# Two blocks of a transformer on one core: modulation chunks placed anew in the feed-forwards and between them

## The reference, cut to what matters

```python
c_act = jax.nn.silu(c)
for i in range(DEPTH):                       # 2
    mod = c_act @ mod_w[i] + mod_b[i]        # 9 * 1024 columns
    sh1, sc1, g1, sh2, sc2, g2, sh3, sc3, g3 = jnp.split(mod, 3 * N_SUB, axis=-1)
    h = modulate(rmsnorm(x, norm_g[i, 0]), sh1, sc1)
    x = x + FFN_RES * g1[:, None, :] * swiglu(h, ffn_w13[i, 0], ffn_w2[i, 0])
    h = modulate(rmsnorm(x, norm_g[i, 1]), sh2, sc2)
    m = pool_ssd_mixer(h, ...) if i % 2 == 0 else mla_mixer(h, ...)
    x = x + g2[:, None, :] * m
    h = modulate(rmsnorm(x, norm_g[i, 2]), sh3, sc3)
    x = x + FFN_RES * g3[:, None, :] * swiglu(h, ffn_w13[i, 1], ffn_w2[i, 1])
```

## Time and profile before

| | |
|---|---|
| median of 3 runs | 1763.58 us (1763.45 to 1764.44) |
| span of the profiled execution | 1764.7 us |
| TensorE busy | 1669.9 us, 95% |
| VectorE busy | 1290.2 us, 73% |
| ScalarE busy | 933.4 us, 53% |
| POOL busy | 86.6 us, 5% |
| first feed-forward, its SiLUs | 54.1 to 238.1 us |
| second feed-forward | 408.8 to 592.2 us |
| third feed-forward | 613.9 to 796.8 us |
| granted TensorE clock 0.50 before 1300 us | 3.4 us each from 82.9, 437.9 and 642.7 us |

### The profile page before, as it was taken

One profiled execution on the slowest core, in us unless ns is written; L12 is line 12 of the kernel. 1 busy time (PEld: TensorE's weight loads), 2 busy tenths in 40 slices (PEclk: granted clock), 3 DMA queues, 4 the chain that ended last, 5 costly groups with the idle time before them and its releaser, 6 DMA issues.

```text
span 1764.7 us, 31956 instructions
## 1 busy us (share of the span) xinstructions
PE 1669.9 (95%) x11230; PEld 1500.6 (85%) x11230; DVE 1290.2 (73%) x2161; ACT 933.4 (53%) x1664; POOL 86.6 (5%) x151
## 2 busy tenths in 40 slices
PE   6899999999999999999999999999988899999998
PEld 5899989888999889998777888898976789988886
DVE  6888888768888888876566666679888565456665
ACT  1544457644444544445575555555467845555553
POOL 2000010300000100000000000000000000000000
PEclk9999999999999999999999999999999999999999
DMA  8888866757888888865433766444633155446561
GB/s 348 311 295 297 306 173 204 156 203 249 300 292 307 236 293 302 294 184 175 131 108 70 240 191 185 148 148 151 186 97 91 49 191 168 143 136 198 191 184 65
DMA packets 123657, 352.76 MB, mean 200 GB/s; under 512 B 9851, under 2 KB 52875, under 8 KB 114225
## 3 DMA queue, kind: packets, MB, share of 16 engines
q1 hardware_dynamic: 108128, 262.18, 46.4%
q10 hardware_dynamic: 12432, 78.65, 13.8%
q0 software_dynamic: 3008, 10.74, 1.9%
HBM read 347.31 MB, written 4.22 MB: 199 GB/s over the span
## 4 chain that ended last, share of the span: by engine, by line
PE 55%; DVE 20%; issue 11%; ACT 8%; DMA 4%; ACTq 1%; POOL 1%; DVEq 0%; POOLq 0%; SPq 0%
PE ps L829 36%; PE ps L1062 8%; PE ps L1063 4%; DVE w_lo L195 4%; DVE arena L358 4%; DVE arena L2680 2%; ACT w_hi L1116 2%; ACT w_hi L189 2%; DVE w_lo L1127 1%; DMA gate_scratch<-gcol 1%; DMA resid<-in_x 1%; DVE resid L1322 1%; DVE act_s L1196 1%; DMA grow<-gate_scratch 1%; ACTq L332 1%
## 5 line engine op out<-in xcount | busy, mean ns | idle before, releaser
L829 PE MATMUL ps<-t_both,w_hi 128*128 128x256 f32 x3952 | 725.9, 285 | 10.1 <-DVE t_both L758 5.7
L829 PEld LDWEIGHTS ps<-t_both,w_hi 128*128 128x128 f32 x3952 | 615.0, 191 | 23.5 <-issue 10.6
L829 PE MATMUL ps<-t_both,w_lo 128*128 128x256 f32 x1976 | 558.5, 283 | 1.3 <-issue 1.3
L195 DVE TENSOR_TENSOR w_lo<-raw,w_hi 128x1024 fp32r<-128x1024 f32 x240 | 288.6, 1222 | 122.6 <-ACT w_hi L189 122.4
L829 PEld LDWEIGHTS ps<-t_both,w_lo 128*128 128x128 f32 x1976 | 376.6, 191 | 0.2
L1127 DVE TENSOR_TENSOR w_lo<-raw,w_hi 128x1024 fp32r<-128x1024 f32 x258 | 313.6, 1221 | 83.0 <-ACT w_hi L1116 82.9
L1116 ACT ACTIVATE w_hi<-raw 128x1024 fp32r<-128x1024 f32 x258 | 268.8, 1053 | 120.2 <-PE ps L829 79.2
L189 ACT ACTIVATE w_hi<-raw 128x1024 fp32r<-128x1024 f32 x240 | 248.2, 1053 | 143.1 <-PE ps L829 99.6
L1062 PE MATMUL ps<-t_both,w_hi 128*128 128x512 f32 x640 | 226.7, 398 | 0.0
L829 PE MATMUL ps<-w_hi,g_hi 128*128 128x512 f32 x440 | 176.8, 402 | 14.4 <-DVE g_lo L1199 11.9
L1063 PE MATMUL ps<-t_both,w_lo 128*128 128x256 f32 x640 | 179.7, 281 | 0.0
(11 more groups left out here) (378 smaller groups left out, 1662.4 us busy)
## 6 DMA issues: line engine op xcount, KB each, us to landing
raw<-in_stream SPq DMA_DIRECT2D x498, 512.0 KB, 4.5
arena<-in_mod_w ACTq DMA_DIRECT2D x72, 1024.0 KB, 7.2
grow<-gate_scratch POOLq DMA_DIRECT2D x6, 512.0 KB, 7.7
u_scratch<-u_keep ACTq DMA_DIRECT2D x1, 3072.0 KB, 36.8
arena<-u_scratch POOLq DMA_DIRECT2D x8, 256.0 KB, 3.3
small<-in_small POOLq DMA_DIRECT2D x1, 1368.0 KB, 11.2
resid<-in_x POOLq DMA_DIRECT2D x1, 1024.0 KB, 18.9
arena<-in_mem POOLq DMA_DIRECT2D x1, 1024.0 KB, 5.4
```

Of the source, the lines that this page charges most:

```text
L195: VE.tensor_tensor(w_lo[:, s, :], raw[:, s, :], w_hi[:, s, :].bitcast(F32), ALU.subtract).then_inc(lo_done, 1)
L829: last = TE.matmul(out, lhs, rhs, start=start and i == 0, stop=stop and i == 2)
```

## The change

Chunks are placed anew. The first feed-forward keeps 4 to 14 in its bodies 0 to 10, but its last body now has the ordinary order of products, and the fold of chunk 14; the chunk's gather, copy and add come behind the narrow product that opens the mixer (`mod_finish`). Chunk 15 starts one split earlier in the mixer's output product (6 to 9 in place of 7 to 9), is folded behind the ninth, and its gather stands behind the tenth block. The second feed-forward has no chunk in body 0, chunks 16 to 25 in bodies 1 to 10, and loads chunk 26 in its last body. The third has no chunk in body 0 (it gathers chunk 25 there), and 26 to 35 in bodies 1 to 10; chunk 35 ends behind the narrow product that opens the second mixer. `late_mod`, `late_load`, `next_mod`, the products in `squares`, the turn in `turn` and `mod_add` are gone. Body 1 of the second and third is written out, and the loop runs over bodies 2 to 9. The first mixer's narrow turn now waits for the copy of chunk 14 (`mod_taken`), since both use bank 7. Nothing of the computation is left out.

```diff
+        def mod_finish(c, place):
+            @block.tensor
+            def _(pe):
+                mod_gather(pe, c, PRE, place)
+            @block.scalar
+            def _(act):
+                mod_take(act, c, PRE, place)
+            @block.gpsimd
+            def _(pool):
+                mod_place(pool, c, PRE)
...
             diag_at[0] = (ready[0, 1], A.n)
             square(1, 1)
             root(1)
-            if late_mod is not None:
-                @block.vector
-                def _(dve):
-                    mod_products(dve, late_mod, (6, 7), turns_at[late_mod])
-
...
-                if late_mod is not None:
-                    @block.tensor
-                    def _(pe):
-                        pe.wait_ge(V.sem, added[QT - 1, 1])
-                        mod_turn(pe, late_mod, place=L)
-
-                    @block.vector
-                    def _(dve):
-                        mod_add(dve, late_mod, turns_at[late_mod], place=L)
-                    if late_load:
-                        mod_first(late_mod + 1, place_free=True, halves=(1,))
...
                 opening = static and i == 0
+                late = static and i == FG - 1
                 for t in range(2):
-                    closing = t == 1 and static and i == FG - 1
-                    if mod is not None and not opening and not closing:
+                    if mod is not None and not opening:
                         mod_products(dve, mod, range(4 * t, 4 * t + 2), turns)
...
-                    if mod is not None and closing:
-                        mod_products(dve, mod, range(4 * t, 4 * t + 2), turns)
-                    elif mod is not None and t == 1 and not opening:
+                    if mod is not None and t == 1 and not opening:
                         mod_products(dve, mod, range(4 * t + 2, 4 * t + 4), turns)
...
-                if mod is not None and not (late and late_mod):
+                if mod is not None:
                     mod_fold(dve, mod, turns)
...
-                owing = 0 < lo and n_mod and lo <= n_mod
+                mod = mod_bodies and lo >= mod_bodies[0]
+                owing = mod_bodies and lo > mod_bodies[0] or call == 2 and lo == 0
...
+            loop_at = 2 if mod_bodies and mod_bodies[0] else 1
+            for i in range(loop_at):
+                if i == 0 and mod_bodies:
+                    blocks["hi"] = h0 + RING
+                emit(i, i + 1)
+            emit(loop_at, FG - 1)
+            if residual is not None:
+                gate_row(residual)
+            emit(FG - 1, FG)
...
         narrow_product(16, ps[2], ahead=4)
+        mod_finish(PRE + FG - 1, L)
         narrow_at, dt_read = A.n, [0]
...
                     pe.wait_ge(A.sem, narrow_at)
+                    pe.wait_ge(mod_taken, FG)
...
-            if between[0] in (7, 8, 9):
+            if between[0] in (6, 7, 8, 9):
                 @block.vector
                 def _(dve):
-                    mod_products(dve, PRE + FG, range(2 * between[0] - 14, 2 * between[0] - 12), turns_at[PRE + FG])
+                    mod_products(dve, PRE + FG, range(2 * between[0] - 12, 2 * between[0] - 10), PRE)
+                    if between[0] == 9:
+                        mod_fold(dve, PRE + FG, PRE)
+            if between[0] == 10:
+                mod_finish(PRE + FG, 0)
...
-        mod_first(PRE + FG + 1, place_free=True, halves=(0,))
+        mod_first(PRE + FG + 1, place_free=True)
...
-        ffn(1, FG, PRE + FG + 1, (mod_at(0, 8), 0.5), next_mod=PRE + 2 * FG + 1)
+        ffn(1, range(1, FG), PRE + FG + 1, (mod_at(0, 8), 0.5), load_on=True)
-        ffn(2, N_MOD - PRE - 2 * FG - 1, PRE + 2 * FG + 1, (mod_at(1, 2), 0.5))
+        ffn(2, range(1, FG), PRE + 2 * FG, (mod_at(1, 2), 0.5))
...
         narrow_product(32, ps[2], ahead=4)
+        mod_finish(N_MOD - 1, L)
```

More of the change, by code:

```diff
@@ L378, in mod_fold, with mod_gather @@
             VE.tensor_reduce(mod_lanes[:, :], mod_swap.rearrange("p (b r) -> p b r", r=32), AX, ALU.add).then_inc(mod_summed, 1)
-        def mod_gather(pe, c, turns):
+        def mod_gather(pe, c, turns, place=0):
             n = c - turns
@@ L393, in mod_take @@
                 rows = slice(32 * g, 32 * g + 32)
-                last = E.activation(mod_sum[rows, :], ps[7][rows, g:16:4], ACT.Copy)
+                last = E.activation(mod_sum[rows, :], ps[7][rows, place + g:place + 16:4], ACT.Copy)
             last.then_inc(mod_taken, 1)
@@ L1017, in _, with ffn @@
                     mod_load(act, half, c)
-        def ffn(call, n_mod, mod0, residual, next_mod=None):
+        def ffn(call, mod_bodies, mod0, residual, load_on=False):
             h0 = blocks["pe"]
@@ L1027, in ffn @@
             fresh = turned["at"] == (V.n, A.n)
-            late_mod = n_mod == FG
-            wide = n_mod == 0
+            wide = not mod_bodies
             sb0 = 2 * (FG - 1) * (call - 3)
-            turns = (PRE, PRE + 2, PRE + 3, None, None)[call]
+            turns = PRE
             def slot(j):
@@ L1243, in _ @@
                         with act.Fori(lo, hi) as i:
-                            act_body(act, i, False, mod_of(i), True, owed_of(i) if owing else None)
+                            act_body(act, i, False, mod_of(i), True, owed_by(i))
                     else:
                         m = mod_of(lo)
-                        act_body(act, lo, True, m, m is not None and lo + 1 < n_mod, owed_of(lo) if owing else None)
+                        act_body(act, lo, True, m, m is not None and (lo + 1 < FG or load_on), owed_by(lo))
                 @block.vector
@@ L1261, in _ @@
                             with pool.Fori(lo, hi) as i:
-                                mod_place(pool, owed_of(i), turns)
+                                mod_place(pool, owed_by(i), turns)
                         else:
-                            mod_place(pool, owed_of(lo), turns)
-            def with_mod(i):
-                return i + mod0
-            def no_mod(i):
-                return None
-            if n_mod:
-                blocks["hi"] = h0 + RING
-                emit(0, 1, with_mod)
-                if n_mod == FG:
-                    emit(1, FG - 1, with_mod)
-                    if residual is not None:
-                        gate_row(residual)
-                    emit(FG - 1, FG, with_mod)
-                else:
-                    emit(1, n_mod - 1, with_mod)
-                    emit(n_mod - 1, n_mod, with_mod)
-                    for i in range(n_mod, FG):
-                        if i == FG - 1 and residual is not None:
-                            gate_row(residual)
-                        emit(i, i + 1, no_mod)
-            else:
-                emit(0, 1, no_mod)
-                emit(1, FG - 1, no_mod)
-                if residual is not None:
-                    gate_row(residual)
-                emit(FG - 1, FG, no_mod)
+                            mod_place(pool, owed_by(lo), turns)
+            loop_at = 2 if mod_bodies and mod_bodies[0] else 1
[7 more added lines that the diff above has]
+            emit(FG - 1, FG)
             blocks["pe"] = h0 + FG * RING
@@ L1294, in ffn @@
             owed[0] = 2
-            if next_mod is not None:
-                mod_first(next_mod, place_free=True, halves=(0,) if late_mod else (0, 1))
             add_residual(residual)
```

51 lines of the change are left out of this document (23 added, 28 removed).

## The result

The changed kernel took **1770.28 us** (median of 17 runs, 1765.97 to 1772.65), the kernel before in the same session 1765.39 us (17 runs, 1763.14 to 1768.21): a ratio of **1.0024, with a 95% interval of 1.0016 to 1.0032**. It is slower, by 4.9 us as a difference of the medians (4.2 us by the ratio). The forecast was 1762.7 us and its range ended at 1767.0. It started from three runs of the kernel before with a median of 1763.58 us; in these 17 runs that kernel itself took 1.8 us more, so 1.8 us of the miss of 7.6 us are not the change's.

The account below looks back on a forecast made before the run. TensorE held over half the last-ending chain, VectorE a fifth, with VectorE pacing bodies that have a chunk. Feed-forwards -4.0, -2.9, +1.5, mixer output +2.2, gathers +0.6, clock +1.7 gave -0.9 us: 1762.7 us, range 1759.0 to 1767.0.

Parts of the forecast that it names:

- First bodies: Second and third feed-forward: no chunk in body 0 removes TensorE's waits; body 10 of the second starts 5.0 us earlier.
- Last bodies: Products and fold now precede the residual adds: 2.3 us later in first feed-forward, 3.2 and 2.9 earlier in second, third.
- Boundaries' length: Behind first and second feed-forward and mixer, late products and turns leave: 4.16 us becomes 3.38, 0.8 us gained each.
- Chunk 15: Mixer's output product: the gather waits 2.7 us for the fold and takes 0.3, so residual adds come 3.0 us later.
- clock term: One 3.4 us stretch at half clock at the mixer's new gather wait, 1.7 us lost; bounds 0 and 1.7.
- Low clock in the boundaries: TensorE's wait for the first turn grows from 1.32 to some 2.15 us in all three; low clock taken as not drawn.
- (d): Longer waits draw the low clock in all three boundaries, 5.1 us on top: +4.2, 1767.8 us; chance 0.1.
- (e): The stall moves with the first products into body 1 or 2 at full size: about +9 us; chance 0.06.

Follow-up runs that it names:

- gather behind the product: Changed kernel with chunk 15's gather, copies and addition moved behind the mixer's row product: 1769.97 us, ratio 1.0023 to the kernel before.
- gather warmed: Changed kernel with 9 small warming products on TensorE ahead of chunk 15's gather, its place kept: 1770.83 us, ratio 1.0020 to the kernel before.

## Why the prediction was wrong

**First bodies: right.** From the boundary to body 10 the second feed-forward gained 5.2 us: TensorE's first product behind the boundary came at 408.3 instead of 401.3 us (7.0 late), body 10's first product at 585.50 instead of 583.73 (1.8 late); forecast 5.0. No wait for the low half was left in bodies 0 and 1, and VectorE kept its period, (585.50 - 445.73) / 8 = 17.47 us.

**Last bodies: right in this execution.** 13.85 us from body 10's first product to the residual adds (forecast 13.45); in the first feed-forward 244.84 - 231.24 against 240.80 - 229.64, 2.4 us more (2.3); in the third the lag behind the kernel before went from 3.36 us (first product behind the boundary, 609.72 against 606.36) to 0.45 us (first residual add, 800.80 against 800.35), 2.9 gained (2.9).

**Boundaries' length: right.** 607.43 - 604.06 = 3.37 us (3.38). **Chunk 15: right.** A wait of 2.67 us (2.7; the clock term names the same wait as 2.55), and one stretch of 3.4 us at half clock behind it, as forecast.

**Low clock in the boundaries: this step failed.** The prediction said "I take the low clock as not drawn there; bounds 0 and 1.7 us each", for waits of "some 2.15 us"; they were 2.23 to 2.60 us. Its rival (d), chance 0.1, had the mechanism and gave +4.2 us, 1767.8. (Its chance of a slower kernel, "(e) and half of (d)", adds up to 0.11, not 0.12.) In place of the forecast's zero, filling these three waits won 3.9 us, and baring those of the kernel before cost 5.3.

What the prediction lacked was the count over executions. In the 14 profiles of this study, between 235 and 830 us, TensorE stood 52 times for 2.0 us or more, and 34 times the low clock was drawn; all 34 stretches of that region stand at such a wait. I had reasoned from two cases, one for and one against, and let the one against stand for three places. The profile of before had more on the side of the low clock: its three stretches ahead of 1300 us, at 82.9, 437.9 and 642.7 us, each stand at a TensorE wait of 2.4 to 2.6 us (2.58, 2.44 and 2.48). The place counts as well: in the boundaries behind the feed-forwards and the first mixer 20 of 27 such waits drew it, in the last bodies, for the low half, 3 of 12, and the gather's 2.67 us drew it in all four profiles that have it.

By the pooled counts a wait of this kind costs at most 34/52 times a mean stretch of 4.2 us at half speed, 0.65 x 2.1 = 1.4 us on top of its length. The changed kernel has four and six of them in its two profiles: 5 x 1.4 = 7.0 us.

**What the removed stretches were worth: less than half of 3.4 us.** The repeated kernel before drew no low clock in body 1 (its granted clock is 1.00 there) and shows what the one at 437.9 us had cost. First products of bodies 1 and 10 on VectorE, in its profile:

```profile
425.52 0.48 DVE L355 TENSOR_SCALAR arena<-arena,cact 128x512 f32<-128x512 f32 x1
...
582.71 0.48 DVE L355 TENSOR_SCALAR arena<-arena,cact 128x512 f32<-128x512 f32 x1
```

157.19 us, against 583.73 - 425.86 = 157.87: 0.7 us for 3.4 us at half speed, since VectorE sets that pace and TensorE catches up. Behind a boundary less is caught up. From the last residual add of the second feed-forward to the third's first chunk product it takes 25.44 us in the changed kernel without a stretch, and 26.57 and 26.60 us in the two variants with a stretch of 3.4 us there (gather behind the product, gather warmed): 1.1 us. The gather's is dearer: from chunk 15's first product to the last residual add behind the mixer 19.28 us with 3.4 us of low clock, 20.73 us with 6.8, and 17.70 us in the warmed variant, which has none and waits as long for VectorE: 1.6 and 3.0 us. So the change took two waits with a cheap stretch (2 x 0.65 x 0.7 = 0.9 us on average) for some five with a dearer one, though none of these costs the full half.

**The landing: a term that was missing.** I costed the chunk's loads against the gate row only, not against products 4 and 5, which now gate a product of TensorE's path. Of the seven profiles with these products ahead of the low half, five show it with more than 0.3 us in all: 3.1, 2.6, 0.8, 3.6 and 2.4 us, (3.1 + 2.6 + 0.8 + 3.6 + 2.4) / 7 = 1.8 us on average. That this time reaches the end of the kernel at its full size isn't shown; the variant made to win it back, products 4 and 5 behind the low half, was no faster.

**The sum again.** Without its clock term the forecast was -0.9 - 1.7 = -2.6 us, with two stretches of 0.7 us in it: -1.2 without any clock. Less 0.9 for what the clock costs the kernel before, plus 1.8 for landings and 7.0 for the clock gives +6.7 us, an upper value. With 1.1 to 1.6 us for a stretch in place of 1.7 the clock term is 4.5 to 6.6 us and the sum +4.2 to +6.3, an estimate from a few profiles. Another way to an upper value: the mean clock fell by 0.0034 in the repeated runs, 0.0034 x 1766 = 6.0 us at most; -1.2 + 1.8 + 6.0 = +6.6. Measured were +4.9 and +5.7 us.

One part stays open. Near the kernel's start, ahead of everything that the change moved, a stretch of low clock at 43 to 45 us stands in 8 of the 11 profiles of the changed kernel and its variants and in none of the three of the kernel before. In seven it is 6.8 us long, and the first chunk product starts at 57.2 to 58.1 us there, against 55.5 to 56.6 in the six profiles without; it goes with TensorE's wait at 41 us, which is 1.5 to 2.1 us in those eight and 1.3 or less in the others. Whether that is chance or an effect of the change no run settles, so up to some 1.5 us of the slowdown may come from there.

Not tried alone were a separate buffer for the last chunk, which would take the landing away by itself, and an earlier gate row (it was 0.88 us late in the warmed kernel's second feed-forward).

The Trainium skill (TensorE: Matmul & The Clock Gate, section Why this matters for your kernels) warns only of idle gaps longer than most of these. The 24 stretches at waits of 2.0 to 2.7 us disagree, and filling gaps of 2.2 to 2.6 us won 3.9 us; the ten waits of 3.2 to 4.1 us, which all drew the low clock, agree.

## What to carry to other kernels

An idle stretch on TensorE has two prices: its length, and the low clock that it may draw. When work moves, add up not only the waits but list every one of 2 us or more before and after, and weigh each with the share that drew the low clock in several profiles; one profile can't tell. Where a wait can't be shortened, small unneeded products inside it can win time, 3.9 us here. All ten waits of 3.2 us and more drew the low clock, and 24 of the 42 shorter ones, so joining two waits is a risk; that it costs time by itself wasn't shown. Count by place too: the same length drew it at one place nearly always and at another seldom. A stretch at half clock is cheap where another engine sets the pace, so ask where a wait stands before moving it.

## What was not expected of the hardware

- Between 235 and 830 us, 34 of 52 waits of 2.0 to 4.1 us on TensorE were followed by (or ended in) a stretch at clock 0.50, which is 1.2 instead of 2.4 GHz, of 3.4 us in 26 cases and 6.8 us in 8. The same wait of the same kernel did and didn't draw it: 2.23 and 2.25 us at the first boundary in two executions; 2.44 to 2.48 us in the first bodies of the kernel before, two of four times in its two profiles. The wait of 2.5 to 2.6 us in the first feed-forward, between 79 and 85 us in all 14 profiles, drew it in 13.
- The run-to-run spread of the kernel before, 1763.0 to 1771.1 us over the 33 runs of one session, goes with the granted clock: executions at 0.994 to 0.995 took 1763.0 to 1764.1 us, those at 0.989 and 0.990 took 1765.4 to 1771.1.
- The load of a chunk's half (1 MB), waited for 0.1 us at most in one profile of the changed kernel, was 0.9 to 1.2 us late three times in the next.
- A low-clock stretch of 3.4 us costs what its place makes of it: 0.7 us in a body that VectorE paces, 1.1 us behind the second feed-forward, 1.6 us in the mixer's output product.
